# Two heads' score matmuls placed side by side, ahead of their mask products, in a two-layer transformer stage

## What is computed

```python
    kb, vb = band(k), band(v)
    scale = HEAD_DIM ** -0.5
    s = jnp.einsum('bnqkgd,bnskd->bnkgqs', qb, kb,
                   preferred_element_type=jnp.float32) * scale
    qi = jnp.arange(BLOCK)[:, None]
    sj = jnp.arange(2 * BLOCK)[None, :]
    rel = qi + BLOCK - sj
    kpos = jnp.arange(nb)[:, None, None] * BLOCK - BLOCK + sj
    mask = (rel >= 0) & (rel < WINDOW_2) & (kpos >= 0)
    s = jnp.where(mask[None, :, None, None], s, -jnp.inf)
    ...
    m = jnp.maximum(jnp.max(s, axis=-1, keepdims=True), sink)
    p = jnp.exp(s - m)
    p = p / (jnp.sum(p, axis=-1, keepdims=True) + jnp.exp(sink - m))
    o = jnp.einsum('bnkgqs,bnskd->bnqkgd', p.astype(v.dtype), vb)
```

## Time and profile before

| | us |
|---|---|
| runs, unprofiled | 2561.84, 2567.66, 2570.46 (median 2567.66) |
| the profiled execution, its own time | 2573.36 |
| its span in the trace | 2571.5 |
| busy in the span: PE / DVE / ACT | 2448.3 / 1287.1 / 879.8 |
| granted clock of PE, mean over the span | 0.948 |

### The profile page before, as it was taken

One profiled execution on the slowest core, in us unless ns is written; L12 is line 12 of the kernel. 1 busy time (PEld: TensorE's weight loads), 2 busy tenths in 40 slices (PEclk: granted clock), 3 DMA queues, 4 the chain that ended last, 5 costly groups with the idle time before them and its releaser, 6 DMA issues.

```text
span 2571.5 us, 30241 instructions
## 1 busy us (share of the span) xinstructions
PE 2448.3 (95%) x11256; PEld 1960.3 (76%) x11256; DVE 1287.1 (50%) x1896; ACT 879.8 (34%) x1405; POOL 182.9 (7%) x137
## 2 busy tenths in 40 slices
PE   7999998979999979999989999999999898999999
PEld 6876787768888857876667888888877677788887
DVE  6456445344443246767344444333877434544433
ACT  4534443343332233323432333223233343433222
POOL 3000021020000020010011000001010001100001
PEclk9999799989999989999589999999999779999999
DMA  5310023112222213210001222323211001222221
GB/s 200 115 50 18 33 94 117 53 66 82 98 98 99 98 49 125 82 66 34 17 34 66 98 96 91 106 99 109 98 67 51 32 1 66 82 98 98 96 100 65
DMA packets 29200, 202.24 MB, mean 79 GB/s; under 512 B 3232, under 2 KB 3872, under 8 KB 5408
## 3 DMA queue, kind: packets, MB, share of 16 engines
q1 hardware_dynamic: 27072, 195.05, 21.4%
q10 hardware_dynamic: 2016, 5.71, 0.6%
HBM read 198.64 MB, written 2.10 MB: 78 GB/s over the span
## 4 chain that ended last, share of the span: by engine, by line
PE 87%; DVE 5%; ACT 4%; issue 4%; DMA 0%; ACTq 0%; POOL 0%; DVEq 0%; POOLq 0%
PE bank L335 23%; PE bank L337 22%; PE bank L336 22%; PE bank L1663 3%; PE bank L1687 2%; PE bank L757 2%; ACT w_hi L256 2%; PE bank L784 1%; PE bank L1676 1%; PE bank L285 1%; PE bank L1664 1%; DVE h L1389 1%; PE bank L773 1%; PE bank L1710 1%; PE bank L1711 1%
## 5 line engine op out<-in xcount | busy, mean ns | idle before, releaser
L335 PE MATMUL bank<-x_hi,w_hi 128*128 128x512 f32 x2080 | 834.8, 401 | 53.3 <-DVE x_lo L326 30.2
L337 PE MATMUL bank<-x_hi,w_lo 128*128 128x512 f32 x2080 | 818.2, 393 | 0.0
L336 PE MATMUL bank<-x_lo,w_hi 128*128 128x512 f32 x2080 | 817.8, 393 | 0.0
L260 DVE TENSOR_TENSOR w_lo<-w_raw,w_hi 128x2048 fp32r<-128x2048 f32 x180 | 414.9, 2306 | 415.7 <-ACT w_hi L256 415.7
L335 PEld LDWEIGHTS bank<-x_hi,w_hi 128*128 128x128 f32 x2080 | 396.1, 190 | 143.8 <-DVE x_lo L326 32.5
L256 ACT ACTIVATE w_hi<-w_raw 128x2048 fp32r<-128x2048 f32 x180 | 344.1, 1914 | 397.5 <-PE bank L337 395.7
L337 PEld LDWEIGHTS bank<-x_hi,w_lo 128*128 128x128 f32 x2080 | 395.2, 190 | 84.7
L336 PEld LDWEIGHTS bank<-x_lo,w_hi 128*128 128x128 f32 x2080 | 396.3, 191 | 81.8 <-issue 2.9
L337 PE MATMUL bank<-f_hi,w_lo 128*128 128x512 f32 x528 | 208.6, 395 | 0.0
L336 PE MATMUL bank<-f_lo,w_hi 128*128 128x512 f32 x528 | 208.6, 395 | 0.0
L335 PE MATMUL bank<-f_hi,w_hi 128*128 128x512 f32 x528 | 208.6, 395 | 0.0
(11 more groups left out here) (308 smaller groups left out, 2525.5 us busy)
## 6 DMA issues: line engine op xcount, KB each, us to landing
w_raw<-w_d SPq DMA_DIRECT2D x184, 1024.0 KB, 4.8
h<-x_d ACTq DMA_DIRECT2D x4, 512.0 KB, 7.7
out_d<-h SPq DMA_DIRECT2D x4, 512.0 KB, 4.9
tab<-rope_d ACTq DMA_DIRECT2D x2, 640.0 KB, 4.1
memT<-mem_d ACTq DMA_DIRECT2D x1, 1024.0 KB, 5.3
stage<-cmask_d ACTq DMA_DIRECT2D x1, 384.0 KB, 8.7
pos_i<-pos_d ACTq DMA_DIRECT2D x1, 256.0 KB, 8.6
gains<-pack_d ACTq DMA_DIRECT2D x1, 228.5 KB, 5.9
```

The source lines that it names most:

```text
L260: dve.tensor_tensor(w_lo[:, u.slot, :], w_raw[:, u.slot, :], w_hi[:, u.slot, :], ALU.subtract).then_inc(lo_ready, 1)
L335: pe.matmul(dst, wh[:, k, cols], hi[:, kx_, 0:width], start=start, stop=False)
L336: pe.matmul(dst, wh[:, k, cols], lo[:, kx_, 0:width], start=False, stop=False)
L337: return pe.matmul(dst, wl[:, k, cols], hi[:, kx_, 0:width], start=False, stop=stop)
```

## The change

In `scores` the mask products leave the loop over heads and get a loop of their own behind it. PE issues the same four matmuls of a job with the same operands, but both heads' query-key products come first and both mask products follow. The semaphore is raised by the same instruction, the last mask product. No other engine's stream is touched, and nothing else in PE's. Lines behind L1663 move down by one: what is L1664 before is L1665 now, L1676 is L1677, and so on.

```diff
@@ -1661,7 +1661,8 @@
                     dst = bank[:, score_bank(j) + e, c0:2 * P]
                     keys = key_rows(lq[:, 8, :], lkx[:, :], e, g)[:, k0:(i + 1) * P]
                     pe.matmul(dst, lq[HD * e:HD * e + HD, tile, i * P:(i + 1) * P], keys, start=True, stop=False)
-                    mm = pe.matmul(dst, ident_b[:, :], mask_b[:, c0:2 * P], start=False, stop=True)
+                for e in range(2):
+                    mm = pe.matmul(bank[:, score_bank(j) + e, c0:2 * P], ident_b[:, :], mask_b[:, c0:2 * P], start=False, stop=True)
                 mm.then_inc(A["scores"], 1)
```

## The result

| | before | after |
|---|---|---|
| runs, unprofiled, median (range), us | 2569.06 (2561.84 to 2575.96), 4 runs | 2528.21 (2525.44 to 2529.73), 4 runs |
| the profiled execution, its own time / span | 2573.36 / 2571.5 | 2529.16 / 2527.4 |
| busy PE / DVE / ACT | 2448.3 / 1287.1 / 879.8 | 2383.6 / 1286.8 / 880.0 |
| mean granted clock | 0.948 | 0.957 |

The ratio is 0.984, with a 95% interval of 0.9811 to 0.9869: faster by 41 us, where 26 were forecast. Three things tell why: what a job's four matmuls take, where PE waits now, and the clock.

The account below looks back on a forecast made before the run. TensorE (PE), busy 95% of the span, was taken to set the pace outside its waits. Passages 15.1 plus overlap 11.3 made 26.4 us, from the median 2567.66 to 2541 us; range 2529 to 2564.

Parts of the forecast that it names:

- The passages: Between 64- and 128-row products: one there-and-back fewer per job, 0.29, 0.42 or 0.31 us, 15.1 us for both passes.
- The overlap: Two heads' neighbouring score products on different array halves partly overlap, saving 11.3 us for both passes.
- the middle: Score products: four records take the time of three by issue order, saving 0.22, 0.42 or 0.11 us per job.
- a whole overlap: Rival: the second head's score product runs wholly beside the first; 37.8 us saved in all, 2529.9 us, chance 0.04.
- The clock pattern, half from 1228 to 1290, stays: Sign expected in the changed profile: the attention's granted clock remains 0.50 from 1228 to 1290 us.
- the clock comes up as well: Rival: denser work raises the half clock from 1243 to 1270 us, 10 us more a pass, 2521 us, chance 0.09.
- the stream gets only about a tenth denser: Argument against the clock rising from 1243 to 1270 us: PE's work there becomes only about a tenth denser.
- The slower rival: Rival: a longer wait before the convolution's sum drops the clock, costing 12 us a pass; 2577 or 2565 us, chance 0.05.
- It decides once that wait is near 2.5 us: The wait ahead of the convolution's sum lowers the clock decisively only when near 2.5 us long.
- The waits: PE's four waits for the copied probabilities were to grow from 12.3 us to some 15.
- Job count and where it lies on the path: Of 32 jobs per pass, 22 save time: 7 at full clock, 8 at half clock, 7 with 128 keys.
- The jobs costed at nothing: The other 10 of 32 jobs stand right ahead of a wait, so their savings only lengthen it.

Follow-up runs that it names:

- kernel 7: Changed kernel, plus first-block attention jobs from 16 on with both branches' mask products behind both score products: 2526.66 us, ratio 0.9834.
- kernel 10: Changed kernel with neighbouring first-block jobs' scores issued in pairs, an earlier job's gate and value products ahead of each pair: 2538.97 us, ratio 0.9875.
- 13: Changed kernel with paired first-block scores, plus useless products ahead of the transposes of steps 6, 12 and 20 of the repeated layer: 2510.31 us, ratio 0.9782.
- kernel 1: Changed kernel, but head 1's score product waits by semaphore until head 0's has ended: 2566.79 us, ratio 1.0001 to before.
- experiment 5: Changed kernel's order, but both score products use the lower 64 rows, leaving head 1's scores out: 2562.92 us, ratio 0.9988 to before.
- kernel 3: Changed kernel with the new order in jobs 13 to 21 of each pass only, the old order elsewhere: 2545.17 us, ratio 0.9909 to before.
- kernel 9: Kernel before, plus eight useless products ahead of the scores of each of jobs 14 and 15: 2558.77 us, ratio 0.9957.
- kernels 4: Changed kernel with the old order in jobs 13 to 21 of each pass, the new order in the others: 2558.96 us, ratio 0.997 to before.
- kernel 14: Changed kernel, plus 12, 15 and 22 useless products ahead of the scores of jobs 6, 12 and 20, in their own banks: 2507.55 us, ratio 0.9767.

## Why the prediction was wrong in size

- **The passages: right.** 0.29 us per there-and-back at full clock was read as left-over time; the version with both products in the lower half measured 0.30. At half clock 0.42 was read and 0.41 measured. The Trainium skill (TensorEngine Tiling (Array Packing), Key Properties) says that a change of the mode drains TensorE; the runs put 0.22 (two columns added between the masks) to 0.30 us on one there-and-back.
- **The overlap: the step that failed.** The prediction took "the middle", with "Four records then take the time of three", because "PE starts matmuls in program order". In the trace head 1's first record does not stand behind head 0's second: the two first records start together, then the two second ones. The whole second product is hidden, and a job saves 0.72, 1.26 and 0.52 us; the rival "a whole overlap" adds up to 0.73, 1.26 and 0.53. It had a chance of 0.04. That is the term that was mis-sized: 11.3 us in the forecast, about 22.5 by the prices measured (2 x 18.8 less the 15.1 of the passages). The page that was set against it (TensorE: Matmul & The Clock Gate, Packing small matmuls, in the Trainium skill) has matmuls in different row groups run concurrently, and the trace agrees: 0.00 to 0.01 us apart. The order of issue was an argument, not a row, and a whole overlap deserved a larger chance.
- **The clock: the second failure.** "The clock pattern, half from 1228 to 1290, stays" is wrong. The rival "the clock comes up as well" (0.09) happened, from about 1242 on, along with the whole overlap. Its argument against was that "the stream gets only about a tenth denser". With the whole overlap a step is a quarter shorter, 2.35 us (1213.38 to 1215.73) instead of 3.07.
- **The slower rival's mechanism happened, in small.** PE reaches the sum sooner, the wait there grew (1.24 to 1.45 us), and the clock fell in the sum. It cost 1.5 us a pass, not 12, because the clock was back up by 1213. "It decides once that wait is near 2.5 us" is also wrong, and the length of the wait alone does not decide at all: behind 1.43 to 1.46 us the sum took about 5.2 us in some passes and 3.67 in others of the same code (kernels 7, 10 and 13), and in kernel 1 a wait of 2.51 us at T1 of the second pass left the clock at full.
- **The waits: right in kind.** They were to grow to about 15 us and grew to 23.4: the savings ahead of each wait do end in it, and more was saved.
- **Job count and where it lies on the path: right as far as it shows.** In the two stages without a change of the clock three jobs and one gave what three and one should. 22 jobs at the measured prices are 18.8 us a pass, of 27.1 and 21.8. The jobs costed at nothing did end in the waits: the one at T3 took up 6.0 us.

With the forecast's own prices for a whole overlap (37.8 us) 2567.66 becomes 2529.9, 1.7 us above the median measured. That this is so near is in part luck: the clock's 8.3 and 3.0 us came on top in the profiled pair, 4.9 us were lost in the rest of the kernel, and the profiled execution of before was 4 to 6 us slower than the medians beside it. Other executions of before, up to 11.5 us faster than the profiled one, had a higher mean clock (experiment 5); kernel 1's profile is such a case (2555.84 us, the fastest of its ten runs; the clock is up from 1256 to 1272 without any overlap).

**What stays open.** What brings the clock up in the middle. It came up with the new order there (change, kernel 3), with useless products ahead of it (kernel 9), and in the one profile of kernel 1 with neither; it did not in kernels 4 and 5. Before's runs spread over 25 us, the change's over 4 in the first measurement and 9 in the second. The mean granted clocks go with that: 0.945 to 0.957 in the 59 runs of before and 0.945 to 0.959 in kernel 1's ten, 0.953 to 0.958 in the change's eight, 0.955 to 0.962 in all of kernels 3 and 9, at most 0.949 in all of kernels 4 and 5. That fits a clock that comes up in the middle in some executions of before and in all of the change. A mean over the whole span doesn't say in which stretch the clock was up, and one profile per kernel doesn't settle it. Why the same wait of about 1.45 us costs the clock in one pass and not in the next is open as well.

## What to carry to other kernels

Products with a contraction of 64 belong in pairs, one in the lower and one in the upper half of the array, issued next to each other, with the full-height work before or behind both: here, with a bank for each, the second cost nothing, float32 with its two records included. Both into one bank was not tried. Count separately what such a reordering saves at passages (here 0.3 us each there-and-back) and by the overlap, and expect the saving ahead of a wait to end in it. Where PE stands still for some us in a stream that is otherwise bound by it, look at the granted clock behind the wait; useless products that fit into the wait and need no wait of their own can win more than a well-meant reordering (kernel 14 against kernel 10). Before a small gain is read off medians, compare the mean granted clocks of the runs: the kernel it is measured against may have had the full clock for longer in some of them.

## What had not been expected of the hardware

- Two float32 products of two records each, on different halves, interleave by record: the starts are 1213.38, 1213.38, 1213.70, 1213.70, though the program issues them head by head.
- The price of a wait lies behind it: 49 products a pass that no one reads made the changed kernel 20.7 us faster (kernel 14), and 16 a pass made the kernel before 13 us faster.
- The clock can stay up behind a short wait or not, with the same stream around it: in kernel 7 the sum takes 3.67 us in one pass and 5.22 in the other, behind waits of 1.46 and 1.44 us.
